# Fetching each partition's expert rows as one 16 KB piece in a mixture-of-experts step

## What is computed

```python
D_MODEL, D_FF, N_EXPERTS, TOP_K = 1024, 1024, 32, 4
logits = h @ router_w + router_b                # h: (tokens, 1024)
top_vals, top_idx = lax.top_k(logits, 4)
gates = softmax(top_vals)
for e in range(32):                              # tokens routed to expert e
    gu = xb @ w_gate_up[e] + b_gate_up[e]        # (n, 1024) @ (1024, 2048)
    g = min(gu[:, :1024], 7); u = clip(gu[:, 1024:], -7, 7)
    act = (u + 1) * g * sigmoid(1.702 * g)
    y = act @ w_down[e] + b_down[e]              # (n, 1024) @ (1024, 1024)
# each token adds its four experts' rows, weighted by its gates, to the residual
```

## Time and profile before

| | us |
|---|---|
| median of three runs | 1907.69 |
| the profiled execution | 1899.69 |
| its span in the trace | 1898.0 |
| PE busy | 1482.2 (78%) |
| VectorE (DVE) busy | 795.5 (42%) |
| ScalarE (ACT) busy | 329.4 (17%) |
| GpSimd (POOL) busy | 116.9 (6%) |
| TensorE weight loads (PEld) busy | 607.4 (32%) |

### The profile page before, as it was taken

The page is one execution under the profiler, slowest core; times in us unless marked ns, Lnnn a source line. Parts: engine busy times, 40 slices in busy tenths (PEclk is TensorE's granted clock), DMA queues, the critical chain, the costliest instruction groups (busy, mean ns, idle before and its releaser), DMA issues.

```text
span 1898.0 us, 34894 instructions
## 1 busy us (share of the span) xinstructions
PE 1482.2 (78%) x13340; PEld 607.4 (32%) x13341; DVE 795.5 (42%) x1156; ACT 329.4 (17%) x771; POOL 116.9 (6%) x178
## 2 busy tenths in 40 slices
PE   3879956678778651899878699999999998699930
PEld 2434423456434320232222133333333322232310
DVE  3597878985877232132313123231321332131305
ACT  2211112222200010012212112121121212121110
POOL 0000010000000005001100000101000011001000
PEclk8999965789978665999999899999999999999965
DMA  9168898878888840599999999998999999899636
GB/s 328 52 192 272 287 322 258 253 239 269 257 291 280 296 167 14 213 417 413 419 413 406 370 368 404 396 416 358 408 377 401 417 418 417 357 419 410 251 141 233
DMA packets 168701, 598.77 MB, mean 315 GB/s; under 512 B 20791, under 2 KB 20837, under 8 KB 135242
## 3 DMA queue, kind: packets, MB, share of 16 engines
q1 hardware_dynamic: 150048, 560.72, 77.7%
q10 hardware_dynamic: 8522, 20.00, 3.1%
q0 software_dynamic: 10064, 17.12, 2.4%
HBM read 589.38 MB, written 25.90 MB: 324 GB/s over the span
## 4 chain that ended last, share of the span: by engine, by line
PE 47%; DMA 25%; DVE 11%; SPq 6%; issue 6%; ACT 3%; POOL 1%; POOLq 0%; ACTq 0%; DVEq 0%
PE bank L1313 15%; DMA wts<-in_w_gate_up 13%; PE bank L1348 8%; PE bank L1039 6%; PE bank L1331 5%; DMA h_tok<-h_rows,v_tok 5%; PE bank L1359 3%; DMA wts<-in_cache_k 3%; DVE wts L1416 3%; SPq L422 3%; SPq L419 3%; PE bank L1186 2%; DVE sc L1419 2%; DMA wts<-in_w_in 2%; PE bank L1302 1%
## 5 line engine op out<-in xcount | busy, mean ns | idle before, releaser
L1313 PE MATMUL bank<-wts,h_T 128*32 128x512 f32 x4096 | 458.4, 603 | 35.1 <-DMA wts<-in_w_gate_up 35.1
L1794 DVE TENSOR_SCALAR q_T<-bank 128x512 f32<-128x512 f32 x32 | 22.1, 692 | 651.3 <-PE bank L1313 651.3
L1313 PEld LDWEIGHTS bank<-wts,h_T 128*32 128x32 f32 x4096 | 126.2, 111 | 348.3 <-issue 291.1
L1348 PE MATMUL bank<-wts,k_T 128*32 128x512 f32 x2048 | 232.0, 603 | 6.4 <-DMA wts<-in_w_down 4.9
L1416 DVE TENSOR_TENSOR wts<-wts,q_b 128x1024 f32<-128x1024 f32 x128 | 158.2, 1236 | 47.5 <-DMA wts<-in_cache_k 46.2
L1419 DVE TENSOR_REDUCE sc<-wts 128x16 f32<-128x1024 f32 x128 | 156.2, 1220 | 4.4
L969 ACT ACTIVATE h_T<-bank 128x512 f32<-128x512 f32 x66 | 36.7, 595 | 644.0 <-PE bank L1302 643.9
L1331 PE MATMUL bank<-wts,h_T 128*32 128x512 f32 x1024 | 123.8, 632 | 23.1 <-DMA wts<-in_w_gate_up 23.1
L1348 PEld LDWEIGHTS bank<-wts,k_T 128*32 128x32 f32 x2048 | 64.7, 111 | 153.0 <-issue 139.5
L1264 PE MATMUL bank<-v_ring,ex 128*2 128x128 f32 x2048 | 90.8, 316 | 18.3 <-DMA v_ring<-in_cache_v 18.3
L1039 PE MATMUL bank<-wts,h_T 128*8 128x128 f32 (+1 forms) x480 | 93.1, 464 | 12.0 <-DMA wts<-in_w_in 5.9
(11 more groups left out here) (257 smaller groups left out, 1300.8 us busy)
## 6 DMA issues: line engine op xcount, KB each, us to landing
wts<-in_w_gate_up SPq DMA_DIRECT2D x128, 2048.0 KB, 13.5
wts<-in_w_down SPq DMA_DIRECT2D x64, 2048.0 KB
wts<-in_cache_k SPq DMA_DIRECT2D x256, 256.0 KB, 3.6
v_ring<-in_cache_v SPq DMA_DIRECT2D x256, 256.0 KB, 3.6
wts<-in_w_in SPq DMA_DIRECT2D x5, 2048.0 KB, 24.1
wts<-y_rows SPq DMA_DIRECT2D x4, 2048.0 KB, 10.7
wts<-in_w_out ACTq DMA_DIRECT2D x1, 4096.0 KB, 19.5
x_in<-in_x_prompt ACTq DMA_DIRECT2D x6, 512.0 KB
```

The lines of the kernel that those rows point to most:

```text
L1313: m = nc.tensor.matmul(PS[part][p0:p0 + 32, :], lhs[:, 32 * b:32 * b + 32], rhs[:, part * F + half * 512:part * F + half * 512 + 512], sta ...
L1348: m = nc.tensor.matmul(PS[4][p0:p0 + 32, :], act_T[0][:, k, a0:a0 + 32], dn_chunk[c][:, k, n * 512:(n + 1) * 512], start=(c == 0 and k == ...
```

## The change

Row 8p+k of the gate-and-up matrix now goes to partition p, in place of row 128k+p. Chunk c takes the rows 8p+2c and 8p+2c+1 of each partition: 2 x 8 KB that lie one behind the other in HBM. A down chunk q takes rows 512q+4p to 512q+4p+3: 4 x 4 KB, one behind the other. So that the products still pair the same rows and columns, the transposes read their data with matching strides: every eighth number (32 B apart) of a gathered row, and every fourth (16 B apart) of a half row of activated values. The number of DMAs, matmuls and transposes, all waits and all buffers stay as they are.

```diff
         xg = h_tok
+        xg_by_k = h_tok[:, :].rearrange("t (p k) -> t k p", k=KT)
         hg_T = h_T
...
                 if c < 4:
-                    src = w_gate_up[0][bass.ds(e, 1), c * 256:(c + 1) * 256, :].rearrange(
-                        "a (k p) n -> (a p) k n", p=P)
+                    src = w_gate_up[0][bass.ds(e, 1), :, :].rearrange(
+                        "a (p k) n -> (a p) k n", p=P)[:, 2 * c:2 * c + 2, :]
                     sp.dma_start(gu_chunk[c], src).then_inc(w_full[c], 16)
                 else:
                     q = c - 4
                     src = w_down[0][bass.ds(e, 1), q * 512:(q + 1) * 512, :].rearrange(
-                        "a (k p) n -> (a p) k n", p=P)
+                        "a (p k) n -> (a p) k n", p=P)
...
                     for k in range(4):
-                        m = pe.transpose(TB[q][:, k * P:(k + 1) * P], xg[:, (4 * q + k) * P:(4 * q + k + 1) * P],
-                                         ident[:, :])
+                        m = pe.transpose(TB[q][:, k * P:(k + 1) * P], xg_by_k[:, 4 * q + k, :], ident[:, :])
...
                     for k in range(4):
-                        m = pe.transpose(TB[part][:, k * P:(k + 1) * P], act_tok[part][:, k * P:(k + 1) * P],
-                                         ident[:, :])
+                        m = pe.transpose(TB[part][:, k * P:(k + 1) * P],
+                                         act_tok[part].rearrange("t (p k) -> t k p", k=4)[:, k, :], ident[:, :])
```

## The result

The changed kernel takes 1955.36 us (median of four runs, 1953.35 to 1960.01) against 1908.91 us for the kernel before in the same comparison (1907.59 to 1912.91): a ratio of 1.0243, 95% interval 1.0218 to 1.0268. It is 2.4% slower. 1958 us and 2.6% were forecast. The profiled executions have spans of 1951.6 and 1898.0 us.

The account below looks back on a forecast made before the run. Weight loads bound small blocks, PE the larger ones, with the gather loop 3 us short of binding small blocks. Terms +81.1 - 30.9 + 0 = +50.2 us on 1907.7 gave 1958 us, range 1900 to 1990.

Parts of the forecast that it names:

- the small blocks: 17 of 32 expert blocks, at most 64 tokens: gather loop becomes the bound, 595.7 us against 514.6, +81.1 us.
- blocks 10, 27, 29 and 30: Larger blocks after small ones find their weights loaded: -13.1, -14.1 and, for 29 with 30, -3.7; together -30.9 us.
- Part 1, the loads: Expert weight loads joined into 16 KB packets: 30.5 to 29.6 us an expert, 0.9 us gained where loads bind.
- the 18 experts: Experts whose loads bind, counted as 9, 6 and 3 in runs ending in blocks 10, 27 and 30.
- Part 2, the turns: Gather packets alternate with weight packets; 18 turns an engine add 5.4 us, small-block landing 10.4 to 15.8 us.
- The tail: Last part of a small block's gather loop, from landing through transposes to the down product's end: taken as 10.1 us.
- The cover for the larger blocks: PE's own 22 us before the next transposes against the gather's 24.0: taken as 0 loss, 30 us as bound above.
- The second rival: The gather does not suffer: loop stays 28.7 us, 18 experts save 0.9 us each, 1892 us; chance 0.14.
- Part 3, the strides: 16 transposes a block load a stationary operand with 32 or 16 B between neighbours: cost taken as 0.
- the bound of 52: Upper bound in us for strided transposes over all blocks, if a load took twice as long and nothing hid it.
- The first four: Rivals: weaker turns, 1915 to 1932 (0.11); gather unaffected, 1892 (0.14); strides cost too, 1970 to 2010 (0.11); nothing joined, 1907 (0.06).
- The fifth: Rival: wider spacing of the partitions' rows slows the weight loads by more than 7%, above 1960 us; chance 0.03.

Follow-up runs that it names:

- The early gather: Changed kernel with the gather of block i+1 issued ahead of the scatter of block i-2: 1889.78 us against 1904.99 before, ratio 0.9917; repeated, 0.9888.
- the strides-only kernel: Kernel before with its own loads but the changed kernel's strided transposes: 1907.44 us against 1906.75, ratio 1.0011.
- the 8 KB form: Changed kernel with every weight load cut in two, same rows, strides and 64 KB spacing: 1901.54 us against 1906.75 for the kernel before, ratio 0.9976.

## Why the prediction was right, and where it was off

**The direction and the size.** +50.2 us were forecast, the spans differ by 53.6, the medians by 46.5. The profiled execution of the kernel before lies 8 us under its median, that of the kernel after 2 us under, so the medians are the fairer comparison. Of the two single terms, the small blocks came out at +82.0 (forecast +81.1) and blocks 10, 27, 29 and 30 at -30.7 (-30.9).

**Part 1, the loads.** Right: joined pieces of 16 KB, 0.615 us each, which make 29.6 us for an expert as forecast. The 30.5 us before were a little low; over 200 us they are 30.7, so the gain is 1.1 us and not 0.9. In the changed kernel that gain is not lost to the DMA engines; it stands in the profile as idle time of theirs (share 0.86 to 0.95 in the small blocks, 1.00 to 1.02 before). The early gather turns it into time. What I did wrong in the experiments is the price of the smaller pieces, read from stretches of 6 and 7 us: 25 us came for 14, where the price over 200 us gives 20, and 15 for 9, where it gives 11. That the 18 experts would stay 18 was never tested by itself.

**Part 2, the turns.** Right: 136 to 136 packets, landings of 14.3 to 15.3 us in the 17 small blocks where 15.8 was forecast. The 0.7 us that the landing is short of it were made up by the rest of the loop. The tail was 11.0 us (886.41 to 897.4) rather than 10.1: when the transposes start, after PE has idled for 7.8 us, the granted clock is 0.50:

```profile
886.41:888.38 1.97, 1.97 (x12) 1.64 (x16) 0.00 (x0) 0.60 (x1) 0.00 (x0) 0.50 1.11 474
```

Eight transposes take 1.97 us there and 1.09 in a larger block at a granted clock of 1.00. The prediction had such a block in view (11.1 us with the clock down) and took 10 for the middle of blocks whose waits were shorter. Two errors of about 0.8 us cancelled in each block; that the sum for the small blocks comes out within 1 us of 81.1 is luck. The cover for the larger blocks held: no wait for `h_tok` in any of them, and gathers there land in 4 to 8 us.

The second rival has the trace against it: single packets of the two queues stand in turn, as the 278 of 283 places above show, and at three sizes of packet the counts are 294 to 256, 183 to 177 and 136 to 136.

**Part 3, the strides.** They cost something, where I took nothing. Eight transposes in a larger block of the kernel after, from the chain: those of gathered rows (32 B stride), then those of activated values (16 B):

```profile
1189.99 1.09 PE bank L1303 x8
...
1201.54 1.17 PE bank L1384 x8
```

1.02 before for each kind, so 0.07 and 0.15 us, 0.2 us for a block that PE binds. For 15 larger blocks that is 3 us, with 1 us for the 17 small ones, whose loop has only the first group. It is of the order of the 2.3 us left over above, and far from the bound of 52; the strides-only kernel can't tell it from nothing. The wider stride costs less than the narrower one, 0.07 against 0.15 us, and no run shows why.

**The rivals.** The first four fell: landings near 15 us, the gather's waits, a few us for the strides, 109,088 packets. The fifth, the spacing, has no effect that shows in the 8 KB form, and the 16 KB packet takes the same 0.615 us.

## What to carry to other kernels

In this kernel larger DMA pieces were faster for their own queue and slower for the small transfer that shared the engines with it. Before making pieces larger, find the small transfers in flight, count their packets on an engine, and multiply by the growth of the big packet (here 18 x 0.30 = 5.4 us, of which 5.0 were measured). If one of them is within that distance of being the bound, move its issue first; here the same change is worth -0.8 to -1.1% with the gather issued early and +2.4% without. And read the price of a packet from a long stretch: 6 us gave 0.8 us an expert for the 4 KB pieces, 200 us gave 1.1.

## What the runs showed of the hardware that I had not expected

A strided load of TensorE's stationary operand takes longer, though the numbers it loads are as many. Duration of a load in ns (min, median, max) for the gathered rows after; before the median was 141:

```profile
L1303 PEld LDWEIGHTS bank<-ident,h_tok x264: 185/204/231, 753.9 to 1849.1; 128*128 128x128 f32 x132
```

The activated values' loads, 16 B apart, have a median of 212. Of these 63 and 71 ns only 9 and 19 reach the pace of the transposes (0.07 and 0.15 us for eight). The rest doesn't show in their pace.

Empty slots are not free either. Of the 288 packets that the scatter and the gather put on q0 from 907 to 922 us, 111 carry a row of 4 KB. The other 177, for empty slots and for the ends of the DMAs, have 4 bytes and take 9 ns, but each takes its turn behind a weight packet all the same, so a gather of few tokens lands no sooner. With 89 rows in scatter and gather together, the one issued at 939.94 lands after 14.9 us; with 128 rows, the one issued at 833.71 after 14.8. And 288 packets are there in larger blocks too (1103.6 to 1134.5 us).
